# Experts' way down wholly as split fp32r products, one Silu instruction, single copies of rows and outputs, and a new order of a step

## The reference, cut to what matters

```
def expert_block(args):              # one block of up to 128 rows of one expert
    xb, e = args                     # xb: 128 x 1024
    gate, up = jnp.split(xb @ w_gate_up[e], 2, axis=-1)      # 1024 -> 2 x 256
    return (jax.nn.silu(gate) * up) @ w_down[e]              # 256 -> 1024
y = zeros.at[tok_sorted].add(y_disp[dest] * w_sorted)        # weighted sum of a token's two rows
```

## Time and profile before

| what | value |
|---|---|
| median of 3 runs | 2841.32 us (2839.97 to 2843.55) |
| the profiled execution's own time | 2841.04 us |
| its span | 2839.1 us |
| mean granted TensorE clock | 0.97 |
| PE busy over the span | 2647.8 us (93%) |
| DVE, ACT, POOL busy | 59%, 49%, 24% |

### The profile page before, as it was taken

How to read it: one execution, slowest core, us unless ns; L and a number is a source line. 1 busy time by engine, 2 the same in 40 slices (tenths; PEclk the granted TensorE clock), 3 DMA queues, 4 the chain that set the end, 5 groups by cost and what they waited for, 6 DMA issues and landing times. The chain is left out here.

```text
span 2839.1 us, 38303 instructions
## 1 busy us (share of the span) xinstructions
PE 2647.8 (93%) x12914; PEld 2085.5 (73%) x12914; DVE 1675.3 (59%) x2334; ACT 1389.1 (49%) x2316; POOL 668.4 (24%) x708
## 2 busy tenths in 40 slices
PE   9999999999998999999799998999949999999980
PEld 7778788787776777776799996777737777777750
DVE  4624525425327677766554444565568888888858
ACT  5334334333325777776311114453417777777753
POOL 0000000000014566664222220000013444444420
PEclk9999999999999999999899999999969999999995
DMA  4263353454443211112553444122369999999978
GB/s 178 90 203 120 116 181 119 135 178 156 147 114 74 46 40 39 40 39 83 166 147 122 122 151 164 60 90 82 119 245 341 373 374 372 375 384 385 378 260 360
DMA packets 168852, 508.69 MB, mean 179 GB/s; under 512 B 40448, under 2 KB 69760, under 8 KB 140576
## 3 DMA queue, kind: packets, MB, share of 16 engines
q1 hardware_dynamic: 150000, 472.56, 48.1%
q0 software_dynamic: 18720, 34.64, 3.2%
q10 hardware_dynamic: 16, 0.00, 0.0%
HBM read 432.21 MB, written 108.33 MB: 190 GB/s over the span
## 5 line engine op out<-in xcount | busy, mean ns | idle before, releaser
L531 DVE TENSOR_TENSOR fr_wl<-fr_raw,fr_wh 128x1024 fp32r<-128x1024 f32 x128 | 156.8, 1225 | 449.3 <-ACT fr_wh L399 448.6
L399 ACT CAST fr_wh<-fr_raw 128x1024 fp32r<-128x1024 f32 x128 | 134.0, 1047 | 491.1 <-PE fr_acc L312 266.5
L2624 DVE TENSOR_TENSOR ex_gl<-ba_raw,ex_gh 128x2048 fp32r<-128x2048 f32 x128 | 293.2, 2292 | 101.3 <-ACT ex_gh L2537 101.3
L1019 DVE TENSOR_REDUCE at_nm<-at_psA 128x1 f32<-128x512 f32 (+2 forms) x320 | 191.2, 608 | 137.1 <-PE at_psA L895 83.0
L2537 ACT CAST ex_gh<-ba_raw 128x2048 fp32r<-128x2048 f32 x128 | 245.2, 1917 | 39.2 <-PEq L2132 39.2
L1103 POOL TENSOR_TENSOR at_pl<-at_pf,at_ph 128x512 fp32r<-128x512 f32 (+1 forms) x160 | 191.8, 1199 | 207.1 <-ACT at_ph L985 206.5
L2474 PE MATMUL ex_psG<-ex_gh,ex_xh 128*128 128x512 f32 x512 | 200.8, 392 | 6.7 <-DVE ex_xl L2629 5.3
L2475 PE MATMUL ex_psG<-ex_gl,ex_xh 128*128 128x512 f32 x512 | 200.3, 391 | 0.0
L2476 PE MATMUL ex_psG<-ex_gh,ex_xl 128*128 128x512 f32 x512 | 200.3, 391 | 0.0
L1079 POOL CAST at_vh<-all_cst 128x32 fp32r<-128x32 f32 x2 | 0.5, 228 | 830.0 <-POOLq L111 830.0
L984 ACT ACTIVATE at_pf<-at_psS 128x512 f32<-128x512 f32 (+3 forms) x240 | 125.3, 522 | 76.9 <-PE at_psS L861 39.8
(11 more groups left out here) (410 smaller groups left out, 6694.2 us busy)
## 6 DMA issues: line engine op xcount, KB each, us to landing
ba_raw<-in_w_exp SPq DMA_DIRECT2D x192, 1024.0 KB, 19.5
fr_raw<-in_w_slabs SPq DMA_DIRECT2D x128, 512.0 KB, 3.7
gates_d<-fr_gst SPq DMA_DIRECT2D x64, 256.0 KB, 4.4
mx_gt<-gates_d SPq DMA_DIRECT2D x64, 256.0 KB, 5.5
cb_ys<-y_d SPq DMA_DIRECT2D x16, 1024.0 KB, 11.4
mx_xr<-in_x SPq DMA_DIRECT2D x8, 1024.0 KB, 7.1
x_d<-mx_xo SPq DMA_DIRECT2D x8, 1024.0 KB, 5.0
xa_xe<-x_d SPq DMA_DIRECT2D x16, 512.0 KB, 4.7
```

The source lines that it names most:

```text
L399: nc.scalar.copy(wh[:, i % 2], raw[:, i % 2]).then_inc(w_hi, 1)
L531: V.tensor_tensor(wl[:, i % 2], raw[:, i % 2], wh[:, i % 2], ALU.subtract).then_inc(w_lo, 1)
L1019: V.tensor_reduce(nm[:, i, c:c + 1], psA[b][:, 0:w], AX, ALU.max, negate=True).then_inc(a_max, 1)
L2624: V.tensor_tensor(gl[:, s, i], raw[:, r, i, :].rearrange("p (k n) -> p k n", k=KD // 2), gh[:, s, i], ALU.subtract).then_inc(w_lo, 1)
```

## The change

The whole way down becomes split products: `dh`, `down_high` and `down_low` take all 2048 columns of the piece, `go_down` makes 12 fp32r products and no f32 one, and the plain copy `hT` goes. Sigmoid and one DVE product are replaced by one Silu on ACT. `psX` and `psY` become one tile each, so `take_x` is one cast and one subtraction of 128 x 1024, and `take_y` one copy. The step has a new order: PE does half 0 of `gate_up`, the two turns, half 1 and then `go_down`; ACT and DVE begin with the way down of b-1, ACT copies `y` of b-2, and both halves of the gate-and-up of b+2 are made in step b. SP takes `gate_and_up(e + 3)` ahead of `way_down(e)`. The last expert's way down has high parts of its own, `spare`, in the place of `gh`, made during the last step. `gate_up` takes the half `i` as an argument. The steps on DVE and the first one follow the same order as on ACT. The cut diff:

```diff
+        spare = s_.at("spare", [P, 2, D], F32R, gh_at)
         gh = s_.sb("gh", [P, 2, 2, KD // 2, 2 * FF], F32R)
         gl = s_.sb("gl", [P, 2, 2, KD // 2, 2 * FF], F32R)
-        sg = s_.sb("sg", [P, 2, FF])
         hm = s_.sb("hm", [P, 2, FF])
-        hT = s_.sb("hT", [P, 2, P])
-        dh = s_.sb("dh", [P, 2, CH], F32R)
-        psX = [s_.ps(f"psX{i}", [P, 4, P]) for i in range(2)]
+        dh = s_.sb("dh", [P, 2, D], F32R)
+        psX = s_.ps("psX", [P, KD, P])
-        psY = [s_.ps(f"psY{i}", [P, CH]) for i in range(2)]
+        psY = s_.ps("psY", [P, 2, CH])
...
-            for j in range(1, RAW + 1):
+            for j in range(RAW):
                 step(j, 0, j, True, True)
...
@@ sync
-            for e in range(2):
+            for e in range(3):
                 gate_and_up(e, e)
             with sp.Fori(0, E // RAW - 2) as t:
                 for r in range(RAW):
-                    gate_and_up(RAW * t + (r + 2), (r + 2) % RAW)
+                    gate_and_up(RAW * t + (r + 3), (r + 3) % RAW)
                     way_down(RAW * t + r, r)
             for e in range(E - 2 * RAW, E - RAW):
-                if e + 2 < E - RAW:
-                    gate_and_up(e + 2, (e + 2) % RAW)
+                if e + 3 < E - RAW:
+                    gate_and_up(e + 3, (e + 3) % RAW)
                 way_down(e, e % RAW)
-            for j in (0, 1, 3, 4, 2, 6, 7, 5):
+            for j in (0, 1, 3, 4, 6, 7, 2, 5):
...
@@ tensor
-            def go_down(b, s, r, nw):
-                pe.wait_ge(r_in[r][2], nw)
-                pe.wait_ge(hcopy, b + 1)
-                pe.wait_ge(yv, b + 1)
+            def go_down(b, r, hi):
+                pe.wait_ge(d_lo, b + 1)
+                pe.wait_ge(h_lo, b + 2)
+                pe.wait_ge(y_taken, b + 1)
                 for k in range(2):
-                    nc.tensor.matmul(psY[1][:], hT[:, k, :], raw[:, r, 2, k * D + CH:k * D + 2 * CH], start=(k == 0), stop=(k == 1))
...
+                    for n in range(2):
+                        c = slice(n * CH, (n + 1) * CH)
+                        lo = raw_lo[:, r, 2, k * D + n * CH:k * D + (n + 1) * CH]
+                        for i, (x_, w) in enumerate(((hTh, hi[:, k, c]), (hTl, hi[:, k, c]), (hTh, lo))):
+                            mm = nc.tensor.matmul(psY[:, n, :], x_[:, k, :], w, start=(k == 0 and i == 0), stop=(k == 1 and i == 2))
                 mm.then_inc(down, 1)
...
             def step(b, t, j, more, more2):
                 s = j % 2
-                gate_up(b, s, b - 1)
-                turn_hidden(b - 1, 1 - s)
+                gate_up(b, s, 0, None if first(b) else b - 1)
+                if not first(b):
+                    turn_hidden(b - 1, 1 - s)
                 if more:
                     turn(b + 1, 1 - s, 16 * (RAW // 2) * t + 16 * ((j + 1) // 2 + 1))
-                go_down(b - 1, 1 - s, (j - 1) % RAW, landed(t, j - 1))
+                gate_up(b, s, 1)
+                if not first(b):
+                    go_down(b - 1, (j - 1) % RAW, dh)
             steps(pe, step)
             turn_hidden(E - 1, 1)
-            go_down(E - 1, 1, RAW - 1, 16 * (E // RAW))
+            go_down(E - 1, RAW - 1, spare[:])
...
@@ scalar
-            def sigmoid(b, s):
+            def gate(b, s):
                 act.wait_ge(used, 2 * b + 2)
-                nc.scalar.activation(sg[:, s, :], psG[s][:, 0:FF], ACT.Sigmoid).then_inc(sig, 1)
+                nc.scalar.activation(hm[:, s, :], psG[s][:, 0:FF], ACT.Silu).then_inc(sig, 1)
...
             weights_high(0, 0, 0, 16)
-            take_x(0, 0, True)
+            take_first_x()
             weights_high(1, 1, 1, 16)
-            sigmoid(0, 0)
-            take_x(1, 1, True)
-            weights_high(2, 0, 2, 16, 0, (0,))
-            down_high(0, 0, 16)
             def step(b, t, j, more, more2):
                 s = j % 2
-                if more:
-                    weights_high(b + 1, 1 - s, (j + 1) % RAW, landed(t, j + 1), b - 1, (1,))
-                sigmoid(b, s)
-                take_h(b - 1)
+                if not first(b):
+                    down_high(b - 1, (j - 1) % RAW, landed(t, j - 1), dh[:])
+                    if not isinstance(b, int) or b > 1:
+                        take_y(b - 2, s, 16 * (RAW // 2) * t + 16 * ((j - 2) // 2))
+                    take_h(b - 1)
+                if more2:
+                    weights_high(b + 2, s, (j + 2) % RAW, landed(t, j + 2), b, (0,))
                 if more:
                     take_x(b + 1, 1 - s)
+                else:
+                    act.wait_ge(r_in[j][2], landed(t, j))
+                    nc.scalar.copy(spare[:], raw[:, j, 2, :].rearrange("p (k n) -> p k n", k=2)).then_inc(d_hi, 1)
+                gate(b, s)
                 if more2:
-                    weights_high(b + 2, s, (j + 2) % RAW, landed(t, j + 2), b, (0,))
-                take_y(b - 1, 1 - s, 16 * (RAW // 2) * t + 16 * ((j - 1) // 2))
-                down_high(b, j % RAW, landed(t, j))
+                    weights_high(b + 2, s, (j + 2) % RAW, landed(t, j + 2), b, (1,))
             steps(act, step)
+            take_y(E - 2, 0, 16 * (E // 2 - 1))
             take_h(E - 1)
             take_y(E - 1, 1, 16 * (E // 2 - 1))
...
@@ vector
             def hidden(b, s):
                 dve.wait_ge(sig, b + 1)
-                V.tensor_tensor(sg[:, s, :], psG[s][:, 0:FF], sg[:, s, :], ALU.mult).then_inc(gt, 1)
-                dve.wait_ge(gt, b + 1)
-                V.tensor_tensor(hm[:, s, :], psG[s][:, FF:], sg[:, s, :], ALU.mult).then_inc(hid, 1)
+                V.tensor_tensor(hm[:, s, :], psG[s][:, FF:], hm[:, s, :], ALU.mult).then_inc(hid, 1)
...
```

More of the change, by code:

```diff
@@ L2314, in _, with experts @@
             link(V.tensor_tensor(wts[:, :, 1:2], wts[:, :, 0:1], gm[:, :, 2:3], ALU.mult))
-def experts(nc, cst, h_d, x3_d, w_exp, y_d, tab, rows, meta, raw, raw_lo, r_in, x3_in, xg, x_in, y):
+def experts(nc, cst, h_d, x3_d, w_exp, y_d, tab, rows, meta, raw, raw_lo, r_in, x3_in, xg, x_in, y, hTh):
     with ExitStack() as ctx:
@@ L2366, in landed, with first @@
             return 16 * t + 16 * (j // RAW + 1)
+        def first(b):
+            return isinstance(b, int) and b == 0
         @block.sync
@@ L2455, in _, with turn, gate_up @@
         def _(pe):
-            def turn(b, s, nx, first=False):
+            def turn(b, s, nx):
                 pe.wait_ge(x_in[s], nx)
-                if not first:
+                if not first(b):
                     pe.wait_ge(x_lo, 2 * b)
                 for k in range(KD):
-                    mm = nc.tensor.transpose(psX[k // 4][:, k % 4, :], xg[:, s, k * P:(k + 1) * P], ident)
+                    mm = nc.tensor.transpose(psX[:, k, :], xg[:, s, k * P:(k + 1) * P], ident)
                 mm.then_inc(turned, 1)
-            def gate_up(b, s, free=None):
-                if free is not None:
+            def gate_up(b, s, i, free=None):
+                if i == 0 and free is not None:
                     pe.wait_ge(hid, free + 1)
[L2469 to L2477, removed]
+                pe.wait_ge(x_lo, 2 * b + i + 1)
+                pe.wait_ge(w_lo, 2 * b + i + 1)
+                for k in range(KD // 2):
+                    f = i * (KD // 2) + k
+                    nc.tensor.matmul(psG[s][:], xh[:, s, f, :], gh[:, s, i, k, :], start=(f == 0), stop=False)
+                    nc.tensor.matmul(psG[s][:], xh[:, s, f, :], gl[:, s, i, k, :], start=False, stop=False)
+                    mm = nc.tensor.matmul(psG[s][:], xl[:, s, f, :], gh[:, s, i, k, :], start=False, stop=(f == KD - 1))
+                mm.then_inc(used, 1)
             def turn_hidden(b, s):
@@ L2604, in more @@
                 weights_high(b, 0, 0, 16 * (b - E) + 16 * (E // RAW + 1))
[L2605 to L2607 removed]
+                act.wait_ge(turned, b + 1)
+                act.wait_ge(used, 2 * b)
+                nc.scalar.copy(xh[:, 0], psX[:]).then_inc(x_hi, 2)
+                down_high(b, 0, 16 * (b - E) + 16 * (E // RAW + 1), dh[:])
+                gate(b, 0)
                 take_h(b)
@@ L2648, in _ @@
             weights_low(0, 0, 0)
-            take_x(0, 0)
+            take_first_x()
             weights_low(1, 1, 1)
-            hidden(0, 0)
-            take_x(1, 1)
-            weights_low(2, 0, 2, (0,))
-            down_low(0, 0)
             def step(b, t, j, more, more2):
                 s = j % 2
-                if more:
-                    weights_low(b + 1, 1 - s, (j + 1) % RAW, (1,))
-                hidden(b, s)
-                take_h(b - 1)
+                if not first(b):
+                    down_low(b - 1, (j - 1) % RAW, dh[:])
+                    take_h(b - 1)
+                if more2:
+                    weights_low(b + 2, s, (j + 2) % RAW, (0,))
                 if more:
                     take_x(b + 1, 1 - s)
+                else:
+                    down_low(b, j, spare[:])
+                hidden(b, s)
                 if more2:
```

(7 more changed lines are left out.)

81 lines of the change are left out of this document (37 added, 44 removed).

## The result

The changed kernel takes 2856.1 us (median of 5 runs, 2854.88 to 2856.67), the kernel before 2841.32 (2839.97 to 2843.55): ratio 1.0051, 95% interval 1.0036 to 1.0065. It is 15 us slower; I had said 2842, with 2850 as the upper end of my range. Its profiled execution has a span of 2854.4 us against 2839.1.

What follows compares the result with a forecast made beforehand. Transfers were taken as the floor, 10.10 us a step, hidden by PE until about step 57. PE's end +0.2 and cold products +0.9 gave +1.1 on 2841.04: 2842 us, range 2837 to 2846, 8 in 10 within 2828 to 2850.

Steps and rivals of the forecast that it cites:

- PE's step: PE's time per expert: 9.67 us before, 9.32 after the change if nothing else holds it.
- its limit: Weight pieces' latency: grows 0.78 us a step up to some 29 us, reached after about 28 steps.
- rival 1: Experts' steps: transfers speed up or one engine's share gets less, PE holds 9.32 us steps; 2813, in part 2827; chance 0.16.
- rival 3: Order within a step does not hold, hand-overs make steps longer than 10.10 us; 2850 to 2870; chance 0.07.
- rival 4: Silu and the casts share no table, so ACT's step is 11.2 us; 2910; chance 0.02.
- DMA: the bytes of a step do not change ... from then on every step takes 10.10 us: Experts' weight transfers: same bytes, so once the latency limit is reached each step takes 10.10 us, PE waiting 0.8.
- The front gain of 3.4 us: First steps: fifth piece issued 4.6 us earlier, ninth landing near 2159.4 instead of 2162.8; bounds 0 and 5.
- The end: Last three steps: way down of 60 lands at 2727.8, PE ends at 2759.2 against 2758.96 before.
- the 0.9 for cold products: PE's wait of 1.9 us near the end: seven cold products would cost 1.7 us more, half taken.
- Both marks: End of the experts: way down of 60 landing after 2730 and the experts ending after 2764 would show rival 2.
- rival 2: The end costs more than the front gives, through the late way down of 60; 2846 to 2850; chance 0.15.
- the estimate of 9.0 us: Fullest DMA engine's step: 256 KB at about 27 GiB/s takes 9.0 us, by which PE would hold the step.

Runs made afterwards that it cites:

- a_way_down_even: The changed kernel, with SyncE issuing the way down of e + 4 only when DVE has made the low part of the way down of e + 1; 2845.1 us.
- a_issue_order_before: The changed kernel with SyncE's issue order of the kernel before: gate-and-up of e + 6, last eight pieces in the old order; 2851.7 us.

## Why the prediction was wrong

Right were the shape and the place. PE's step came down, to 9.43 and not 9.32: the 24 products of gate-and-up, now in two parts, take 5.62 us (2241.39 to 2244.24 and 2247.04 to 2249.81) where they took 5.47, the twelve of the way down 2.80 and not 2.76, the transposes 0.08 less. The latency grew to its limit (27 to 30 us; I had 29), reached some 20 steps in instead of 28; from there ACT's `dh` waits for the DMA and PE for what is left, at full clock. Silu (0.39 us, one table load at 2139.0 us and none later in the stage) and the copies (1.01 for `y`) came as counted. Rivals 1, 3 and 4 didn't come.

**The step that failed** is "DMA: the bytes of a step do not change ... from then on every step takes 10.10 us". I took a rate measured in one order of issues as a property of the transfers. It was 10.69 in steps 5 to 15 and 10.29 in the late ones, 12.1 us in all; with one issue moved (a_way_down_even) it is 10.21 and 10.09, and 611.8 over all. With the floor thus restored the kernel takes 2845.1, 3 us above the forecast.

**The front gain of 3.4 us did not come.** The fifth issue was earlier by 2.4 us (2140.5 instead of 2142.86; I had 4.6), but pieces 7 and 8 were later (2151.1 and 2154.8 instead of 2149.0 and 2151.1), and the ninth landed at 2164.5, not 2159.4. I had followed one piece of a step and not the three.

**The end** shows that the rest of the sum held. The way down of 60, the 177th piece of the stage, I had land at 2727.8, and the experts' last product end 31.4 us behind it. Its issue, its landing time and the last product:

```profile
2713.60 0.51 SPq L2375 DMA_DIRECT2D ba_raw<-in_w_exp  x1
```

```profile
ba_raw<-in_w_exp SPq DMA_DIRECT2D x1, 1024.0 KB, 29.3
```

```profile
2774.10 0.39 PE L2499 MATMUL ex_psY<-ba_raw_lo,ba_hTh 128*128 128x512 f32 x1
```

It landed at 2742.9, 15.1 us late, and PE ended at 2774.5, 31.6 behind it; the 0.9 for cold products hardly shows. The 15.1 are the front gain of 3.4 that didn't come, 1.3 of a later first issue, and 10.4 of transfers: from the first issue to the landing of the 177th piece it takes 615.1 us, before 604.7 (2731.2 less 2126.46). Both marks of rival 2 were passed (2730 and 2764), but not for its reason, since the last steps ran as laid out.

**The wrong reading under it.** DMA share 0.99 at 377 GB/s looked like a full resource. It was a mean over engines of which four were far behind the other twelve. I had even set down the fixed partitions per engine of the Trainium skill ("DMA: Bandwidth & Descriptors", section "The descriptor swizzle"), by which the 64 valid rows fall on eight of them, and used only the estimate of 9.0 us, which the trace refuted, instead of asking whether 10.1 was the floor of the fullest few. Why four and not eight are far behind isn't shown. Two smaller readings were off and change no number: the two pieces that give 10.10 us are half 1 of gate-and-up of experts 10 and 60, not way downs, and one slice ahead of the experts has 245 GB/s, not at most 203. Nearest to the truth was rival 1's "one engine's share gets less", for which 2813 to 2827 was worked out; the change didn't do that, the routing's edit does (2823.1).

**Open.** Why closely issued pieces cost the full engines anything, with 10 to 25 us of work queued in front of them, is not shown. Nor is the longest gap the whole law: a_issue_order_before has the longest (7.6) and yet the best late pace (10.02), and the two kernels with the most even issues run their late steps at 10.16 and 10.18 and have transfer times of 620 (they also hold each piece back until an earlier one has landed, so their queues are shorter). A moved issue also stands elsewhere against the gather and the scatter of the rows; no run tells this apart from its distance to the other weight pieces. What is shown is that the moment of an issue matters by itself, not by which rule.

## What to carry to other kernels

Before you take a transfer rate as a floor, ask which DMA engines set it, by when each has landed its part: where a gather fills only the low partitions, spreading its rows cost a few half-width compares in the routing and took 33 us (2856 to 2823). A floor read from a trace belongs to its order of issues; a reordered step needs the times of *all* its issues laid out, and moving one wait of the issuing engine is a cheap thing to try, in both directions. A gain on PE under a DMA floor isn't lost: it pays as soon as the floor is low enough (16 us here).

## What the runs showed of the hardware

- Spacing of issues: the same pieces, bytes and products, one issue moved by 2.0 us took 11 us away (2856.1 to 2845.1), one moved by 3.5 us added 20 (2841.2 to 2860.9). With the rows on all engines the time stays (2823.1 and 2825.6, 2839.5 and 2839.0), the latency doesn't (17.5 and 14.2 us, 7.3 and 12.9).
- 392 GB/s with a DMA share of 1.00 in a stretch of 280 us, against 377 at 0.99 with rows on half the partitions; the weights still land every 9.72 us only.
- One issue 2.0 us later in each step, and the last piece lands at 2740.8 us instead of 2752.8.
- GpSimd's indirect DMA instruction takes 3.03 us (scatter) or 2.70 (gather) when a full-width subtraction of DVE (2.29 us) is already running as it starts, and 1.02 or 1.05 otherwise, also when the subtraction starts 0.05 us behind it. This holds for all 122 of the changed kernel from 2130 to 2750 us, 83 of them slow; of the kernel before's 123 two are slow (1.8 and 2.0 us). In the changed kernel no engine on the path waits for it.
